# Indirect transfers of token rows and TensorE transposes in place of a one-hot gather, in the expert layer of a two-block network

## The reference

```python
def moe_swiglu(h, w_router, wg, wu, wd):
    xt = h.reshape(-1, d)                                  # 256 tokens x 1024
    top_v, top_i = lax.top_k(xt @ w_router, TOP_K)         # 2 of 8 experts
    gates = jax.nn.softmax(top_v, axis=-1)
    comb = jnp.sum(one_hot(top_i, 8) * gates[..., None], axis=1)
    for e in range(N_EXPERTS):
        y = y + comb[:, e:e + 1] * swiglu(xt, wg[e], wu[e], wd[e])

def swiglu(x, wg, wu, wd):                                 # 1024 -> 3584 -> 1024
    return (jax.nn.silu(x @ wg) * (x @ wu)) @ wd
```

## Time and profile before

| | us |
|---|---|
| median of three runs | 1778.37 (1778.29 to 1779.61) |
| the profiled execution | 1779.35 |
| its span in the profile | 1777.6 |
| PE busy | 1747.0 (98%) |
| DVE busy | 1411.9 (79%) |
| ACT busy | 1159.8 (65%) |
| POOL busy | 87.7 (5%) |
| expert layer, first pair's first product to the last pair's last one | 443 to 1408 |

### The profile page before, as it was taken

How to read it: one execution, slowest core, us unless ns; L and a number is a source line. 1 busy time by engine, 2 the same in 40 slices (tenths; PEclk the granted TensorE clock), 3 DMA queues, 4 the chain that set the end, 5 groups by cost and what they waited for, 6 DMA issues and landing times.

```text
span 1777.6 us, 25814 instructions
## 1 busy us (share of the span) xinstructions
PE 1747.0 (98%) x9175; PEld 1482.3 (83%) x9175; DVE 1411.9 (79%) x1583; ACT 1159.8 (65%) x1416; POOL 87.7 (5%) x137
## 2 busy tenths in 40 slices
PE   7999999999999999999999999999999999999998
PEld 7988888898888888888888888888888798878886
DVE  8864454697898998999989999999999887656555
ACT  5644444464777777778777777777777656544554
POOL 0000000001800000000001000000000001000000
PEclk9999999998999999999999999999999999999999
DMA  9555555544899999999999999989999834335520
GB/s 336 165 182 190 188 189 189 168 164 150 325 376 364 395 371 357 373 378 380 376 350 396 395 366 365 378 317 373 384 348 388 292 119 159 127 122 165 164 95 36
DMA packets 211858, 486.92 MB, mean 274 GB/s; under 512 B 13413, under 2 KB 14644, under 8 KB 211780
## 3 DMA queue, kind: packets, MB, share of 16 engines
q1 hardware_dynamic: 209984, 480.02, 75.4%
q0 software_dynamic: 1152, 4.19, 0.6%
q10 hardware_dynamic: 644, 1.63, 0.2%
HBM read 482.67 MB, written 3.15 MB: 273 GB/s over the span
## 4 chain that ended last, share of the span: by engine, by line
PE 92%; DVE 5%; ACT 1%; issue 1%; DMA 0%; ACTq 0%; POOL 0%; POOLq 0%; DVEq 0%
PE ps L1846 84%; DVE wlo L1062 2%; PE ps L2137 1%; DVE arena L1520 1%; PE ps L2099 1%; PE ps L2100 1%; DVE arena L1053 1%; ACT whi L536 0%; PE ps L2289 0%; PE ps L1990 0%; PE ps L2303 0%; PE ps L1938 0%; PE ps L2033 0%; PE ps L2346 0%; PE ps L2070 0%
## 5 line engine op out<-in xcount | busy, mean ns | idle before, releaser
L1062 DVE TENSOR_TENSOR wlo<-raw,whi 128x1024 fp32r<-128x1024 f32 x910 | 1070.4, 1221 | 243.9 <-ACT whi L536 243.3
L536 ACT ACTIVATE whi<-raw 128x1024 fp32r<-128x1024 f32 x910 | 913.0, 1053 | 450.2 <-PE ps L1846 448.4
L1846 PE MATMUL ps<-whi,ya 128*128 128x512 f32 x2272 | 727.4, 393 | 2.6 <-DVE ya L1053 1.4
L1846 PEld LDWEIGHTS ps<-whi,ya 128*128 128x128 f32 x2272 | 426.8, 188 | 91.3 <-issue 2.1
L1846 PE MATMUL ps<-wlo,ya 128*128 128x512 f32 x1136 | 442.9, 390 | 0.0
L1846 PE MATMUL ps<-whi,yh 128*128 128x512 f32 x896 | 285.8, 390 | 0.0
L1846 PEld LDWEIGHTS ps<-wlo,ya 128*128 128x128 f32 x1136 | 213.7, 188 | 42.4
L1846 PEld LDWEIGHTS ps<-whi,yh 128*128 128x128 f32 x896 | 168.2, 188 | 35.6 <-issue 0.6
L1846 PE MATMUL ps<-hhi,whi 128*128 128x256 f32 x656 | 188.3, 287 | 2.7 <-DVE hlo L1124 2.2
L1846 PE MATMUL ps<-hlo,whi 128*128 128x256 f32 x656 | 185.8, 283 | 0.0
L1846 PE MATMUL ps<-hhi,wlo 128*128 128x256 f32 x656 | 185.8, 283 | 0.0
(11 more groups left out here) (366 smaller groups left out, 1166.4 us busy)
## 6 DMA issues: line engine op xcount, KB each, us to landing
raw<-in_moe_w_gate SPq DMA_DIRECT2D x112, 1024.0 KB, 7.2
raw<-in_moe_w_up SPq DMA_DIRECT2D x112, 1024.0 KB, 7.4
raw<-in_moe_w_down SPq DMA_DIRECT2D x112, 1024.0 KB, 7.2
raw<-in_even_w_in SPq DMA_DIRECT2D x21, 1024.0 KB, 5.2
raw<-in_w_in SPq DMA_DIRECT2D x20, 1024.0 KB, 5.9
raw<-in_odd_w_in SPq DMA_DIRECT2D x16, 1024.0 KB, 5.6
raw<-in_ffn_w_gate SPq DMA_DIRECT2D x14, 1024.0 KB, 5.1
raw<-in_ffn_w_up SPq DMA_DIRECT2D x14, 1024.0 KB, 5.2
```

What stands on the lines that cost most here:

```text
L536: act.activation(hi_of(u)[:, n], raw[:, c % RAW, n], ACT.Copy).then_inc(w_hi, 1)
L1062: dve.tensor_tensor(lo_of(u)[:, n], raw[:, c % RAW, n], hi_of(u)[:, n].bitcast(F32), ALU.subtract).then_inc(w_lo, 1)
L1846: ins = pe.matmul(o, s, m, start=first and n == 0, stop=last and n == 2, skip_group_check=True)
```

## The change

After `overflow`, POOL scales both token tiles by their norm factor into XG (two tensor_scalar of 128x1024) and stores them in the new memory tensor `x_rows`, once. It waits for the two stores to land (`y_back`, which is why `add_rows` now counts from 32 more), and goes on with `two_rows`.

In the last step of a pair's first job TensorE makes the numbers of the tokens in the next pair's slots: `slot_tokens`, four matmuls of SR with the token numbers TOK, two columns each. DVE copies them to the integer tile `slot_of`. POOL waits for that (`m_idc`) and issues two indirect transfers that fetch 2 x 128 rows of 4 KB from `x_rows` to XG (`slots_in`). At the pair's end `gather_rows` turns these rows with 16 transposes in place of the 32 matmuls. This holds for the gathers that follow pairs 0, 1 and 2. The gather ahead of pair 0 and the one in the register loop, after pair 3, are as before. Some semaphores are merged (`pool_done`), with the same waits.

```diff
+            def token_rows():
+                for i in range(NT):
+                    link(pool.tensor_scalar(XG[:, i, :], HTOK[:, i, :], rst[:, i:i + 1], None, ALU.mult))
+                    pool.dma_start(x_rows[P * i:P * (i + 1), :], XG[:, i, :]).then_inc(sem("y_back"), 16)
+                pool.wait_ge(sem("y_back"), 32)
+
+            def slots_in(done):
+                pool.wait_ge(sem("m_idc"), done)
+                for s in range(2):
+                    pool.indirect_dma_start(XG[:, s, :], None, x_rows[:, :],
+                                            bass.IndirectOffsetOnAxis(ap=slot_of[:, s:s + 1], axis=0)).then_inc(sem("xe_in"), 16)
+
             def rows_out_and_back():
                 for j in range(STORED):
+                    if j % 2 == 0:
+                        slots_in(j // 2 + 1)
                     pool.wait_ge(sem("m_yhi"), j + 1)
...
+                slots_in(STORED // 2 + 1)
...
                 if k == 3:
                     overflow()
+                    token_rows()
                     two_rows()
                     rows_out_and_back()
...
                 moe_step(dd, last=True)
+                if isinstance(pair, int):
+                    dve.wait_ge(sem("m_idx"), pair + 1)
+                    dve.tensor_copy(slot_of[:, :], ps[:, 6, 0:4].rearrange("p (s n) -> p s n", s=2)[:, :, 0]).then_inc(sem("m_idc"), 1)
                 if not stored:
                     y_lo(j0)
...
+            def gather_rows(k):
+                pe.wait_ge(sem("xe_in"), k * 32)
+                for c in range(KD):
+                    for s in range(2):
+                        o = S * (c % 2) + P * s
+                        ins = pe.transpose(ps[:, (5, 6, 1, 7)[c // 2], o:o + P], XG[:, s, P * c:P * (c + 1)], ident[:, :])
+                    if c % 4 == 3:
+                        ins.then_inc(sem("m_gth"), 1)
+
+            def slot_tokens(k):
+                pe.wait_ge(sem("m_s"), k + 1)
+                for s in range(2):
+                    for i in range(NT):
+                        ins = pe.matmul(ps[:, 6, 2 * s:2 * s + 2], SR[:, i, P * s:P * (s + 1)], TOK[:, i, :], start=s == 0 and i == 0,
+                                        stop=s == 1 and i == 1, skip_group_check=True)
+                ins.then_inc(sem("m_idx"), 1)
...
                 de = pe.snap(dp + (2 * NG - 1))
                 turn_h(de)
-                gather(pair + 1)
+                if isinstance(pair, int):
+                    gather_rows(pair + 1)
+                else:
+                    gather(pair + 1)
                 moe_down(U_MOE + 4, de, de, False, True)
```

More of the change, by code:

```diff
@@ L103, in build @@
         row_of = sb("row_of", [P, 2 * NT], I32)
+        slot_of = sb("slot_of", [P, 2], I32)
+        x_rows = nc.dram_tensor("x_rows", (S, D), F32, kind="Internal").ap()
         y_rows = nc.dram_tensor("y_rows", (STORED * P, D), F32, kind="Internal").ap()
@@ L114, in ar @@
                 **dict(zip("abc", shape)))
+        XG = ar(6176, 2, D)
+        TOK = yb[:, 4064:4068].rearrange("p (i n) -> p i n", i=NT)
         def gbv(o, *shape):
@@ L391, in _ @@
             ins.then_inc(s_const, 1)
+            link(pool.iota(sm[:, 108:112].rearrange("p (i n) -> p i n", i=NT), pattern=[[P, NT], [0, 2]], base=0, channel_multiplier=1,
+                           allow_small_or_imprecise_dtypes=True))
+            pool.tensor_copy(TOK, sm[:, 108:112].rearrange("p (i n) -> p i n", i=NT))
             def rstd(k, n, scale):
@@ L485, in _ @@
                                                  gbv(2768, 16).unsqueeze(2).to_broadcast([P, 16, 64]), ALU.mult)
-                    ins.then_inc(sem("s_skip"), 1)
-                    pool.wait_ge(sem("s_skip"), 1)
+                    ins.then_inc(sem("pool_done"), 1)
+                    pool.wait_ge(sem("pool_done"), 2)
                     pool.wait_ge(sem("s_yq"), 8)
-                    pool.memset(SCT[0], 0.0).then_inc(sem("sct_zero"), 1)
+                    pool.memset(SCT[0], 0.0).then_inc(sem("pool_done"), 1)
                     pool.wait_ge(sem("s_yo"), 1)
-                    pool.memset(SCT[1], 0.0).then_inc(sem("sct_zero"), 1)
+                    pool.memset(SCT[1], 0.0).then_inc(sem("pool_done"), 1)
                 if k == 3:
@@ L495, in _ @@
                     pool.wait_ge(sem("x_half"), 10)
-                    pool.tensor_tensor(HTOK[:, 0, :], X[:, 0, :], BG, ALU.mult).then_inc(sem("x_gain0"), 1)
+                    pool.tensor_tensor(HTOK[:, 0, :], X[:, 0, :], BG, ALU.mult).then_inc(sem("pool_done"), 1)
                 if k > 8:
@@ L715, in _ @@
             for i in range(NT):
-                act.wait_ge(sem("r_step" if i else "x_gain0"), 1)
+                act.wait_ge(sem("r_step" if i else "pool_done"), 1)
                 act.activation(hhi[:, 1024 * i:1024 * (i + 1)], HTOK[:, i, :], ACT.Copy, scale=rst[:, i:i + 1]).then_inc(sem("htok_hi"), 1)
@@ L1351, in _ @@
             dve.wait_ge(sem("r_step"), 2)
-            dve.wait_ge(sem("r_pos"), 1)
+            dve.wait_ge(sem("r_log"), 2)
             R = ps[:, 4, 0:24].rearrange("p (i e) -> p i e", i=3)
@@ L1446, in add_rows @@
             def add_rows(i):
-                dve.wait_ge(sem("y_back"), 32 * (i + 1))
+                dve.wait_ge(sem("y_back"), 32 * (i + 2))
                 for k in range(2):
@@ L1589, in y_out @@
                 dve.wait_ge(sem("s_yq"), 4 * i + 4)
-                dve.wait_ge(sem("s_skip"), 1)
+                dve.wait_ge(sem("pool_done"), 2)
                 tt(YS[:, i, :], YS[:, i, :], ps[:, 6:8, :].rearrange("p b n -> p (b n)"), ALU.add).then_inc(sem("s_ye"), 1)
@@ L1595, in scores @@
                 dve.wait_ge(sem("g_sc"), i + 1)
-                dve.wait_ge(sem("sct_zero"), i + 1)
+                dve.wait_ge(sem("pool_done"), i + 3)
                 for r in range(2):
@@ L2077, in _ @@
             pe.matmul(ps[:, 4, 16:24], ones[:, :], CH[:, 0, :], start=True, stop=False)
-            pe.matmul(ps[:, 4, 16:24], ones[:, :], CH[:, 1, :], start=False, stop=True).then_inc(sem("r_pos"), 1)
+            pe.matmul(ps[:, 4, 16:24], ones[:, :], CH[:, 1, :], start=False, stop=True).then_inc(sem("r_log"), 1)
             keep_busy(3, 6)
@@ L2154, in _, with moe_step @@
             npairs = pe.value_load(tab[0:1, 5:6], min_val=NE // 2, max_val=NJMAX // 2)
-            def moe_step(dd, s, first=False, last=False, place=None, scat=None, stored=None):
+            def moe_step(dd, s, first=False, last=False, place=None, scat=None, stored=None, tokens=None):
                 pe.wait_ge(sem("m_silu"), dd + 1)
                 moe_in(U_MOE + 4, dd, 0, s)
+                if tokens is not None:
+                    slot_tokens(tokens)
                 if place is not None:
@@ L2185, in job_pair @@
                     moe_step(pe.snap(dp + g - 1), 0)
-                moe_step(pe.snap(dp + (NG - 1)), 1, last=True)
+                moe_step(pe.snap(dp + (NG - 1)), 1, last=True, tokens=pair + 1 if isinstance(pair, int) else None)
                 moe_step(pe.snap(dp + NG), 1, first=True, scat=scat1, stored=stored1)
```

## The result

| | before | changed |
|---|---|---|
| median of 18 runs, us | 1779.24 | 1784.02 |
| lowest to highest | 1778.16 to 1779.61 | 1778.32 to 1785.89 |
| profiled execution / span | 1779.35 / 1777.6 | 1782.98 / 1781.2 |

The ratio is 1.0024, with a 95% interval of 1.0018 to 1.0030: slower by a quarter of a percent. The spread says more than the median. The runs of before lie within 1.5 us, those of the changed kernel within 7.6, and its fastest run is as fast as before's. Each run comes with its mean granted clock, and they line up: the run of 1778.32 has 0.997, those near 1782.1 have 0.995, those near 1784.5 have 0.993, the slowest 0.992.

What follows compares the result with a forecast made beforehand. TensorE bounds the expert layer almost without a break, but waits for HTl at pair ends. Terms 0.0 + 1.35 + 0.1 + 0.1 = +1.55 us on the median 1778.37 gave 1779.9, rounded to 1780.0; range 1777.5 to 1785.0.

Steps and rivals of the forecast that it cites:

- the likeliest case: Whole kernel: small additions with no gain from the exchange, 1780.0 us; the forecast had 62%, and same 70%.
- The rival with the lowered clock: Pair ends: 4.3 us without a product lowers TensorE's clock, 1.95 us per fall, 1781.9 to 1785.8; 23%.
- The exchange brings nothing: Three pair ends: 16 transposes for 32 matmuls save 2.2 us each, but TensorE waits for HTl; 0.0 us.
- slot_tokens: Pairs 0 to 2, between two products: four small matmuls, 0.45 us with handover, nothing hiding them; +1.35 us.
- POOL and DVE: POOL's new chain is hidden; DVE's slot_of copy and its delay during the scalings may come through, +0.1 us each.
- my bound of 2.65: POOL's scalings: a large POOL operation takes 2.65 us beside DVE.
- the 0.1 us for the scaling: DVE delayed beside POOL's two scalings, losing 0 to 3.3 us of its time; +0.1 us, bounds 0 and +0.9.
- the 0.1 us for DVE's copy: DVE's slot_of copy, hidden in pairs 0 and 1, may come through in pair 2; +0.1 us, bounds 0 and +0.2.
- The transfers: 1 MB stored near 475 us and three 1 MB fetches leave weight loads in time; 0 us, upper bound +1.0.
- one stretch in which the clock had held: Layer's end, 1413.03 to 1417.17: 16 transposes between two rests, 4.1 us, with the granted clock at 1.00.

Runs made afterwards that it cites:

- putting the hidden tile first: Changed kernel with one weight unit's split at each pair's end moved behind the hidden tile's split on ACT and DVE; 1774.22 us, ratio 0.9967.
- control: The changed kernel run once more, unaltered, beside three other follow-up runs; 1784.06 us, ratio 1.0027.
- the moved split: Kernel before, with one weight unit's split moved behind the hidden tile's at each pair's end on ACT and DVE; 1777.65 us, ratio 0.9994.

## Why the prediction was right or wrong

The range (1777.5 to 1785.0) holds the measured 1784.0, but the likeliest case, 1780.0 and no measurable change, did not come. The rival with the lowered clock did. Of the 4.0 us between 1780.0 and 1784.0, 0.9 are the base: the forecast stood on a median of three runs, 1778.37, and the median of 18 is 1779.24.

- **The exchange brings nothing: right.** Forecast 0.0 with a rest of some 2.2 us; measured 1.96 us of rest at each end, released by DVE's `yh`, and 4.31 us from `turn_h` to the product in both kernels. The reading of two rows that meet within 0.06 us carried it, and putting the hidden tile first showed it.
- **slot_tokens: right.** 1.35 us forecast; pairs 0 to 2 grew by 1.15, and by 1.17 with these matmuls alone.
- **POOL and DVE: the price of one step was wrong, its effect not.** The scalings took 3.83 and 4.18 us, over my bound of 2.65. DVE lost about 0.6 us in each (5.26 for four, where four took 4.62 before; 2.93 for two and not 2.36). TensorE lost nothing that shows: pair 0 grew by 0.41 us as pair 1 by 0.39, and the 0.1 us for the scaling did not come. Nor did the 0.1 us for DVE's copy: pair 2 grew by 0.35, and the wait that would have shown it is 0.9 us in both kernels. The Trainium skill (SBUF — State Buffer, Who interferes with whom) says that the first of the two to issue has the shared port for its whole instruction and shuts the other out. In the trace no DVE row lost a whole POOL row: the loss of 0.6 us lies beside POOL rows of 3.83 and 4.18. Whether POOL's rows were stretched by waiting for DVE's isn't shown, since none ran without DVE beside it. The first fetch was issued at 573.5 and not near 565, as DVE's copy stands behind its low parts of that step and ran at 572.5. That was still 99 us ahead of the transposes, and no fetch took longer than 9.5 us to land.
- **The transfers: right.** Keeping all of them and only the old gather gave 1780.8, with pairs as long as those of the kernel with the small matmuls alone.
- **The clock: the mechanism right, the chance far too low.** I gave it 23%, arguing from one stretch in which the clock had held. That stretch had rests of 0.85 and 0.66 us with transposes between; the new one has 1.96 us of rest in one piece. Right ahead of it lay a rest of 2.37 us (until 1410.92) in which the clock held as well, and which I did not weigh. The run with 39 transposes and no rest held the clock, and the one with 3.49 us of rest lost it behind all three ends. The step that failed is that I added transposes and rest into one length (4.3 us) and compared that with 4.1. Rest alone doesn't settle it either, since the same rest was followed by a fall at one pair end of three in one profile and at two of three in the other. What decides in which is open. A fall cost 1.6 to 1.7 us and lasted 3.4, where I had 1.95 and 3.9.
- **The layer's end: missing from the sum.** I had used its rests as evidence that the clock holds, from one profile. The second profile of before falls there. The stretch accounts for 1.72 us of the difference between the two profiles. The small matmuls alone raised the median by 2.3 us, 1.1 more than the pairs grew, and a fall at the layer's end is the only thing in that profile to put it down to. That the changed kernel falls there in more runs than before does is argued from this and not counted.

Open is how the whole 4.8 us of the median divide between pair ends and layer's end, since only single executions have a profile. The kernels whose pause was filled or absent, with `moe_down` where it was, were 2.8 to 4.4 us faster than the control's 1784.06. That is the share of the pair ends only if the layer's end fell equally often in all of them, and it did not in their profiles (none, 3.4 and 6.8 us).

## What to carry to other kernels

Before shortening a piece on the bottleneck engine, look up what becomes ready while it runs: the next wait may end at the same moment, and then only moving both pays (here 0.0 us for the transposes and 0.8 for the moved split in the lengths of the pairs, and 5 in the median for both). A rest that takes the place of work on TensorE can cost more than the work did, if the clock falls behind it. Where the rest can't be removed it can be filled: of a loss of 4.8 us, products gave back 2.8 and identity transposes 4.4. Judge a change of this size by many runs and the spread of the granted clock, not by one profile.

## What the runs showed of the hardware that I had not expected

- 39 transposes in one piece (4.3 us) kept the granted clock at 1.00 at all three pair ends of the profiled execution, while the same stretch with 20 transposes and 1.96 us of rest lost it behind one or two of three.
- Leaving out 14 of 16 transposes at each of three pair ends made the kernel 3.7 us slower (1787.8 beside 1784.06, five and seven runs).
- The same rest did and did not lower the clock: 1.96 us behind one or two of three pair ends, and 2.37 us at the layer's end in one of two profiles of before.
- The clock stays low for 10.2 or 13.6 us at the router, in two executions of the same kernel. At the layer's end, 970 us later, the profiles have no fall, one of 3.4 us or one of 6.8 us, with `moe_down` behind pair 3 starting within 1.1 us of the same place in four of them (none at 1402.81, 3.4 us at 1402.80, none at 1403.04, 6.8 us at 1403.85).
